# Norm tiles written while the last slab before them is still being multiplied: a two-layer encoder step on one core

## The reference, cut to what matters

```python
def rmsnorm(x, g):
    xf = x.astype(jnp.float32)
    y = xf * lax.rsqrt(jnp.mean(xf * xf, axis=-1, keepdims=True) + EPS)
    return (y * g.astype(jnp.float32)).astype(x.dtype)
...
        x = x + y.astype(x.dtype)
        x = x + cross_attend(rmsnorm(x, p['norm_cross'][l]), mem_k[l], mem_v[l], p['x_wq'][l], p['x_wo'][l])
        x = x + squared_relu_mlp(rmsnorm(x, p['norm_mlp'][l]), p['mlp_w_up'][l], p['mlp_w_down'][l])
```

## The kernel before, in words

| place | norm i | slabs before (read `xnh`/`xnl`) | slabs after (read the new ones) |
|---|---|---|---|
| 1 | 1 | `rs_out` 0 to 3 | `xq` of layer 0 |
| 2 | 2 | `xo` 0 to 3 of layer 0 | MLP up of layer 0 |
| 3 | 4 | `ml_out` 0, 0 to 3 | `xq` of layer 1 |
| 4 | 5 | `xo` 0 to 3 of layer 1 | MLP up of layer 1 |

## Time and profile before

### The profile page before, as it was taken

The page is one execution under the profiler, slowest core; times in us unless marked ns, Lnnn a source line. Parts: engine busy times, 40 slices in busy tenths (PEclk is TensorE's granted clock), DMA queues, the critical chain, the costliest instruction groups (busy, mean ns, idle before and its releaser), DMA issues.

```text
span 2356.1 us, 39080 instructions
## 1 busy us (share of the span) xinstructions
PE 2216.0 (94%) x15879; PEld 2068.4 (88%) x15879; DVE 1270.7 (54%) x2185; ACT 361.7 (15%) x655; POOL 1220.9 (52%) x1185
## 2 busy tenths in 40 slices
PE   7978888999999999999999998999989999999996
PEld 7977777997999999999999985587679799999996
DVE  6698887432554361757557734672634246345263
ACT  4211212212200000021202122331312220000001
POOL 5546677632665565666666640022145166656552
PEclk8988999998999999999999998999899899999998
DMA  5212324320222222223433324442231022222221
GB/s 186 90 54 73 134 95 153 143 72 24 84 73 89 87 75 89 71 103 124 158 147 136 143 84 145 178 160 90 94 137 61 32 77 77 85 90 72 89 87 43
DMA packets 38186, 235.84 MB, mean 100 GB/s; under 512 B 4512, under 2 KB 7584, under 8 KB 12712
## 3 DMA queue, kind: packets, MB, share of 16 engines
q1 hardware_dynamic: 21600, 154.15, 18.6%
q10 hardware_dynamic: 16456, 79.80, 8.9%
HBM read 200.05 MB, written 33.89 MB: 99 GB/s over the span
## 4 chain that ended last, share of the span: by engine, by line
PE 77%; DVE 17%; issue 2%; ACT 2%; POOL 1%; DMA 0%; DVEq 0%; ACTq 0%; POOLq 0%
PE psum L508 61%; PE psum L538 14%; PE psum L524 1%; DVE hl L1920 1%; DVE xnl L1445 1%; DVE hh L1916 1%; DVE tm L1613 1%; DVE xc L1985 1%; DVE CA L1626 1%; POOL wlo L460 1%; DVE ss L1430 0%; DVE hr L1909 0%; DVE hs L1912 0%; DVE C L2211 0%; ACT pr L1185 0%
## 5 line engine op out<-in xcount | busy, mean ns | idle before, releaser
L458 POOL TENSOR_SCALAR whi<-raw 128x512 fp32r<-128x512 f32 x584 | 423.1, 725 | 1046.2 <-PE psum L508 1013.3
L460 POOL TENSOR_TENSOR wlo<-raw,whi 128x512 fp32r<-128x512 f32 x584 | 801.9, 1373 | 48.7
L508 PE MATMUL psum<-xnh,whi 128*128 128x288 f32 (+1 forms) x2816 | 622.2, 299 | 42.4 <-DVE xnl L1445 17.5
L508 PE MATMUL psum<-xnl,whi 128*128 128x288 f32 (+1 forms) x2816 | 616.3, 297 | 0.0
L508 PE MATMUL psum<-xnh,wlo 128*128 128x288 f32 (+1 forms) x2816 | 616.0, 297 | 0.0
L508 PEld LDWEIGHTS psum<-xnh,whi 128*128 128x128 f32 x2816 | 463.2, 191 | 52.1 <-issue 39.5
L508 PEld LDWEIGHTS psum<-xnl,whi 128*128 128x128 f32 x2816 | 463.1, 191 | 0.0
L508 PEld LDWEIGHTS psum<-xnh,wlo 128*128 128x128 f32 x2816 | 463.0, 191 | 0.0
L508 PE MATMUL psum<-hh,whi 128*128 128x288 f32 x1024 | 219.1, 295 | 2.1 <-DVE hl L1920 2.1
L508 PE MATMUL psum<-hl,whi 128*128 128x288 f32 x1024 | 218.7, 294 | 0.0
L508 PE MATMUL psum<-hh,wlo 128*128 128x288 f32 x1024 | 217.2, 293 | 0.0
(11 more groups left out here) (402 smaller groups left out, 2697.9 us busy)
## 6 DMA issues: line engine op xcount, KB each, us to landing
raw<-in_w SPq DMA_DIRECT2D x146, 1024.0 KB, 4.7
C<-in_C ACTq DMA_DIRECT2D x4, 1024.0 KB, 5.2
o_cp<-mvt ACTq DMA_DIRECT2D x4, 1024.0 KB, 3.9
o_cs<-C ACTq DMA_DIRECT2D x4, 1024.0 KB, 4.8
t_xc<-xc ACTq DMA_DIRECT2D x3, 1152.0 KB, 7.2
t_z<-mv ACTq DMA_DIRECT2D x3, 1152.0 KB, 4.2
t_q<-mq ACTq DMA_DIRECT2D x3, 1152.0 KB, 4.2
t_k<-mk ACTq DMA_DIRECT2D x3, 1152.0 KB, 4.2
```

Source lines behind the costliest of these rows:

```text
L458: pool.tensor_scalar(whi[:, s, c], raw[:, s, c], 1.0, 1.0, ALU.mult, ALU.mult).then_inc(S("slab_hi"), 1)
L460: ins = pool.tensor_tensor(wlo[:, s, c], raw[:, s, c], whi[:, s, c].bitcast(F32), ALU.subtract)
L508: ins = pe.matmul(bank(g, 2 * m + b)[:, 0:t1 - t0], W[wi][:, kk, m0 + m, :], r[:, kk, t0:t1], start=(at_first and wi == 0 and r is rh), st ...
```

## The change

TensorE signals a new semaphore `xn_tile_free` behind the last matmul of each tile kk of slab 3, except the last tile (`group_done` says that). 7 signals at 4 places are 28. ScalarE's `high` waits for its own tile's signal, and for the whole slab only at tile 7. VectorE's `low` of tiles 0 to 5 now stands ahead of the adding of slab 3; before it was that of tiles 0 and 1. `out_slab(0, 3)` now takes its tiles in the order 0 to 7, before 4 to 7 and then 0 to 3.

```diff
+XN_BY_TILE = (1, 2, 4, 5)
...
             def project(g, n, rh, rl, kts=DT, m0=0, ms=2, wait=None, turn=None, first=True, halves=((0, HALF), (HALF, T)),
-                        order=None, start=True, stop=True, close=True):
+                        order=None, start=True, stop=True, close=True, tiles_freed=False):
...
+                    if tiles_freed and kk != order[-1]:
+                        ins.then_inc(S("xn_tile_free"), 1)
...
-                project(GR["rs_out", i], SL["rs_out", i], xnh, xnl, wait=None if i else s5_half)
+                project(GR["rs_out", i], SL["rs_out", i], xnh, xnl, wait=None if i else s5_half, tiles_freed=i == 3)
...
-                    project(GR["xo", l, i], SL["xo", l, i], xnh, xnl,
+                    project(GR["xo", l, i], SL["xo", l, i], xnh, xnl, tiles_freed=i == 3,
...
-            for i in range(1, 4):
+            for i in range(1, 3):
                 out_slab(0, i)
+            out_slab(0, 3, order=range(DT), tiles_freed=True)
...
-                if i and kks[0] == 0:
+                if i and i not in XN_BY_TILE and kks[0] == 0:
                     group_ready(act, GR[XN_BEFORE[i]])
                 for kk in kks:
+                    if i in XN_BY_TILE and kk == DT - 1:
+                        group_ready(act, GR[XN_BEFORE[i]])
+                    elif i in XN_BY_TILE:
+                        act.wait_ge(S("xn_tile_free"), 7 * XN_BY_TILE.index(i) + kk + 1)
                     x_tile(i, kk)
...
                     if j == 2:
                         add_squares(i, (4, 5))
-                        low(i, gain, (0, 1))
-                low(i, gain, range(2, 8))
+                        low(i, gain, range(6))
+                low(i, gain, (6, 7))
                 add_squares(i, (6, 7))
```

## The result

After the change: 2339.82 us (median of 6 runs, 2337.93 to 2343.88); before, on the same chip: 2356.32 (6 runs, 2354.53 to 2358.49). The ratio is 0.9933, with a 95% interval from 0.992 to 0.9946. The profiled execution took 2338.77 us. One later execution of before took 2487.48 us at a granted clock of 0.831, where every other execution has 0.963 or more; it is left out wherever runs are compared.

What follows compares the result with a forecast made beforehand. PE was taken to bound the kernel, busy 94% of the span. Four intervals shrinking from 64.72 to 55.44 us gain 9.28, signals and other terms zero: 2355.86 - 9.3 = 2346.6 us, range 2344.0 to 2351.5.

Steps and rivals of the forecast that it cites:

- the four places: Where PE, after slab 3, waits 1.8 us for `xnl`; the four intervals together take 64.72 us before.
- The wait for the whole slab goes to tile 7: At each place the interval becomes one undisturbed slab plus the matmuls on `ss`, 13.86 us: 9.28 us gained over four.
- Tiles 0 to 5: At place 1 their six `low` are done near 459.7, 7 us before PE wants tile 5.
- POOL's split: POOL's work during slab 3, slowed 0.9 us by DVE, ends at 457.4, before PE wants it at 458.83.
- A: Rival: the signals inside slabs drain PE's pipeline, 4.6 of 9.3 us go back, 2351.2; 7%.
- B: Rival: DVE and POOL exclude each other, the split ends 2.2 us after slab 3, 2355.5; 4%.
- C: Rival: POOL loses to every queued DVE operation, PE waits 5.4 us for weights at each place, 2368.4; 3%.
- the rule of whole instructions: Skill's rule: DVE with two SBUF inputs and GpSimd exclude each other for a whole instruction, the loser blocked.
- D: Rival: ACT is held till slab 3 ends by something other than the removed wait, 2355.9; 3%.
- E: Rival: half is given back, by tile 6 coming late or a later wait fixed in time, 2351; 3%.
- Closing a stall of 1.8 us gives nothing more back there: PE's clock stays at 2.4 GHz through place 1 with its stall, so no further gain was counted.
- What comes after a place is shifted as one: Behind each place PE's groups release ACT, DVE and POOL, so no further gain or loss was counted.

Runs made afterwards that it cites:

- signals: Changed kernel with a signal behind every tile of every slab, some 917 more, for which nobody waits: 2341.2 us, ratio 0.9925.
- before_again: The kernel before, unchanged, measured and profiled once more: 2356.12 us, ratio 1.0.
- before_3: The kernel before with three more matmuls on `ss` (1.0 us a place) at places 1 and 3: 2355.41 us, ratio 0.9987.
- before_busy_att: The kernel before with 4 and 9 spare matmuls in two idle times of PE in each attention: 2350.99 us, ratio 0.9966.
- norms_1_4: The kernel before with the change at places 1 and 3 only, ahead of the attentions: 2346.32 us, ratio 0.9961.
- norms_2_5: The kernel before with the change at places 2 and 4 only, ahead of the MLPs: 2351.31 us, ratio 0.997.
- after_3: Changed kernel with three more matmuls on `ss` (1.0 us a place) at places 1 and 3: 2341.56 us, ratio 0.9936.
- after_8: Changed kernel with eight more matmuls on `ss` (2.6 us a place) at places 1 and 3: 2349.24 us, ratio 0.9967.
- after_again: The changed kernel, unchanged, measured and profiled once more: 2340.39 us, ratio 0.9936.
- before_busy_all: The kernel before with 13 spare matmuls in each attention and 4 in each of the four stalls at tile 0: 2350.31 us, measured again 2352.81.

## Why the prediction was right and wrong

**Right:** the direction, the four places and the mechanism. "The wait for the whole slab goes to tile 7" and its sum, 9.28, came out at 9.65; the difference is the three matmuls on `ss`, which take 0.98 us without a stall ahead of them and not 1.08. Tiles 0 to 5 were ready at 460.18 (459.7 forecast), the adding at 460.11 (459.7), tile 7 at 465.7 (465.0), POOL's split took 10.58 us (10.6). Of the rivals none occurred. A is refuted by `signals`. B and C, that POOL is shut out by DVE: its split ended at 457.39, 1.8 us before slab 3, as the rates of the earlier trace rows had given; the rule of whole instructions, which the prediction sets against its rates, isn't borne out here. D and E: the waits are gone, and nothing was given back.

**Wrong:** two terms that were set to zero. They are the step that failed, and they made the range too narrow on the good side.

*"Closing a stall of 1.8 us gives nothing more back there."* This was read off, one place of one execution. In others the same stall is followed by some 3.5 us at 1.2 GHz, which makes the interval 17.3 instead of 16.1 to 16.4. It happened at none of the four places in before, at two in `before_again`, two in `before_3` (places 2 and 3, where 18.05 holds 1.0 of extra work) and three in `before_busy_att`: 0, 2.1, 1.8 and 3.3 us per execution, 1.8 on average. With the two places of `norms_1_4` and the two of `norms_2_5` that keep the stall it is 9 of 20 places. With the stall gone or filled it happened at none of the 40 such places in the table.

*"What comes after a place is shifted as one."* For work released by PE's groups that is so: from the end of place 1's interval to the first attention it is 14.9 us in all fifteen profiled executions, and from the attention to place 2 51.4 to 51.5. The clock isn't shifted along. The attention has idle time of its own. The 64 matmuls behind the 4.49 us take 13.1 to 18.0 us, counted to the start of the projection behind them, and 11.8 with the idle time filled. So 1.3 to 6.2 us are lost in every unfilled attention. The scores behind the 1.85 us take 7.14 or 8.83 us. What comes out differs between executions of one kernel.

Over the three kernels with the old schedule at places 1 and 3 and no extra matmuls, the two attentions add up to 150.4, 144.7 and 150.3 us, mean 148.5; over the four with the new one to 143.1, 144.9, 144.6 and 143.1, mean 143.9: 4.6 less, though single executions overlap (144.7 and 144.9). The three executions with extra matmuls narrow it: 149.4 in `before_3`, 148.0 and 143.9 in `after_3` and `after_8`; with them the means are 148.7 and 144.6. With the attentions filled the gain from the change falls from 17.2 us to 13.25, which is the same term by another way: 4, give or take 3.

So: 9.65 for the intervals, about 2 for the low stretches behind the four stalls, about 4 to 4.6 by way of the attentions, together 16, where 16.5 and 17.2 were measured. The first is simply the change; the second comes with it, as the stall is gone; the third is luck of this program, and nothing says that it would have the same sign in another (`after_3` has a 77.0). What decides how long a low stretch is, and why the attentions come out shorter with the change, stays open. The time since the program's start doesn't decide it: PE reaches the first attention at 489.5 us in before, at 489.2 in `norms_1_4` and at 489.1 in `after_again`, and needs 75.3, 72.5 and 72.5 us. The runs show that the low stretches differ between executions and that they vanish when PE has no idle time.

## What to carry to other kernels

A stall of TensorE costs its length and, in some executions, more in matmuls at 1.2 GHz behind it: here nothing or about 1.2 us behind 1.8, and 1.3 to 6.2 behind 4.49. One profile can miss it, so price a stall from several executions, and give the range room on the side of the gain. Where an idle stretch can't be closed, a few spare matmuls in it are worth trying: here 13 in each attention gave some 2.6 us on top of the change, and 6.6 without it. More isn't always better: with 16 further ones a stall of 4.5 us came up elsewhere. When a kernel is changed far ahead of such a stretch, look at the granted clock there before a difference is put down to the edit, and at the busy time of PE: the same count of matmuls with less busy time is the sign.

## What was unexpected of the hardware

- The clock: the same idle time of 1.8 us was followed at place 2 by a slab of 13.4 us or of 14.5, and the same 4.49 us by 64 matmuls in 14.0 or 18.6 us. Two executions of the very same kernel, before and `before_again`, differ so.
- The pace of undisturbed slabs at a granted clock of 1.00 has two values as well: place 1 takes 13.45 us in `norms_1_4` and `after_again` and 13.78 in after; 300 matmuls take 39.28 us before, 0.131 each, and 396 in after 53.05, 0.134 each. No row shows a cause.
- With 42 spare matmuls, all in idle time, PE stood still elsewhere for 4.5 us and again for 0.5 to 1.1, waiting for nothing that the profile shows. That came in both profiled executions of `before_busy_all`, and in no other kernel, not even those with 26 spare matmuls. Whether the amount of code is the reason stays open.
